# Four transformer layers on one core: later transposes, a second bank for the modulation products, and another order of loads and norm sums

## The chip, the cores and the metric

One core of one Trainium2 chip runs the whole program. The metric is the device time of one execution in microseconds (us), the median of the runs shown. TensorE (PE in the profile), VectorE (DVE), ScalarE (ACT), GpSimd (POOL) and SyncE (SP) are the engines of the core; each has its own queue of instructions.

## The reference, cut to what matters

256 latent tokens `x` and 256 context tokens `ctx`, 2048 wide, go through two layers with modulation, and the latent tokens then through two more. All in float32.

```python
# layers 0 and 1 (l = 0, 1)
mod = silu(c) @ w_mod[l] + b_mod[l];  shift, scale, gate = split(mod, 3)      # for x
cmod = silu(c_ctx) @ w_mod[l] + b_mod[l]                                      # the same for ctx
h = rmsnorm(x, norm_g[l]) * (1 + scale) + shift                              # hc from ctx
u = h @ w_in                                                                 # also uc
y = concat([mixer_1(u), mixer_2(u)]) * silu(u_gate)
x = x + gate * (y @ w_o[l])                                                  # ctx too, in layer 0
# layers 2 and 3
h = rmsnorm(x, norm)
u = h @ w_in
y = concat([mixer_1(u), mixer_2(u)]) * silu(u_gate)
x = x + y @ w_out
```

The mixers are eight kinds of attention (a to h in the kernel): a and b in layer 0, c and d in layer 1, e and f in layer 2, g and h in layer 3. Mixer e picks its keys by an indexer: sixteen small query heads `iq`, rotated, are multiplied with one key head `ik`, and the best 64 keys of each query are kept.

## The kernel before

The weights (some 390 MB) are streamed once. The unit of streaming is a **group**: 256 rows of a weight matrix, 512 columns wide, 0.5 MB. SP loads it into one of `RAW` = 6 buffers `raw`; ACT copies it, rounded, to `w_hi` (line 1046); DVE subtracts to get the rest, `w_lo` (line 1321); both lie in rings of `SPLIT` = 4. The two together stand for the float32 weight. A group is split `AHEAD` = 3 groups before its use, and its ring place is free when TensorE is done with the group four before it.

TensorE works on a group in **quanta**. For an activation product (kinds `u`, `gate`, `lat`, `res`) a quantum is one tile of 128 tokens: 2 rows of K times 3 products (lines 1851 to 1853: hi by hi, hi by lo, lo by hi), 6 matmuls of 512 columns into one of four banks `pp0` to `pp3`. A group has as many quanta as its chunk has token tiles, 4 in layer 0, 2 later. For a modulation product (kind `mod`) a group is one quantum of 4 matmuls (lines 1846, 1847), 4 rows of output in bank `Y`. A **chunk** is 512 columns of output over all K, 8 groups as a rule; `T` is its number of token tiles.

The order of everything is a table of slots. `Work.layers` writes the list of quanta, one to a slot (1644). `Plan.schedule` puts all other work at slots of that list: `evac` (the copy out of a bank, and for a gate chunk the Silu, line 1111), `store`, `cols` (modulation rows turned to columns, line 1863, in bank `O`), `bias`, the attention of each head (`attend`), `x_turn` and `y_turn` (activations transposed by TensorE, then split to `hT_hi` by ACT and `hT_lo` by DVE), `gated` (the multiplication of `y` by the Silu of the gate, line 1368). Each engine walks the slots in order and issues what is its own, at TensorE the events of a slot ahead of its quantum. Where an operand comes from another engine it waits on a semaphore, with all that is queued behind it. `Plan.turns` gives each use of a PSUM bank its turn; a use waits until the turn before is freed.

The places that the change touches:

- **Start.** `setup` of ACT issues the loads of `x` and `ctx` (2 MB each) into `xy`; SP issues the constants, `c`, `c_ctx` and the groups. The squares of `x` (`sq_x`, line 1118) are at slots 6, 8, 10 and 12. Modulation chunks scale0_n and shift0_n (n = 0 to 3) come as pairs, 16 groups; behind the pairs n = 1, 2, 3 come 2, 2 and 4 groups of `b_q0`, the first activation chunk. Four `x_turn` of layer 0 (line 1883) start 2 slots behind each shift0_n.
- **Modulation.** Each chunk adds up in bank `Y`; the next one waits until ACT has copied it to `rows` (line 1084).
- **Layer 0 to 1.** The chunk out0_3 has groups 0 to 7 with tiles 0 to 3 each; the square sums of the new `x`, the root on POOL (line 979) and the scaled identity (`diag`, line 1408) come at its end; then `x_turn` of layer 1 (line 1888).
- **Gated rows.** In layers 1 to 3, `y_to_columns` puts `gated` one slot behind a gate chunk, and the two `y_turn` (line 1912, bank `pp3`) one and two slots behind that. There are 12 such places with two `y_turn` each. The columns made are used in the out chunks, which start behind the fourth gate chunk.
- **Indexer.** `i_rope` (lines 1510 to 1513) rotates `iq` on DVE at slots base+10 to base+16, `i_turn` (line 2031, bank `pp3`) transposes it from base+15, `ik_turn` (line 2038) at base+16, `i_dots` from base+21.

Of the kernel before, what the change touches and what calls it, by code (L numbers as in the profile page):

```python
# [111 lines left out]
class Chunk:  # L112

    def __init__(self, name, kind, w, c0, W, T, ks=None, lhs="h", dst=None, dcol=None, layer=0, ycol=None, block=None, row=None, scaled=None):
        self.name, self.kind, self.w, self.c0, self.W, self.T = name, kind, w, c0, W, T
        self.ks = list(range(KT_)) if ks is None else ks
        self.lhs, self.dst, self.dcol, self.layer, self.ycol = lhs, dst, c0 if dcol is None else dcol, layer, ycol
        self.block, self.row, self.scaled = block, row, scaled
        self.groups = []

class Group:

    def __init__(self, n, ch, j, q0):
        self.n, self.ch, self.j, self.q0 = n, ch, j, q0
        self.ks = ch.ks[GROUP * j:GROUP * j + GROUP]
        self.quanta = 1 if ch.kind == "mod" else ch.T
        self.q1 = q0 + self.quanta

class Work:

    def __init__(self):
        self.groups, self.slots, self.chunks, self.C = [], [], [], {}
        self.layers()
        self.NQ = len(self.slots)
        self.NS = self.NQ + 40
        self.banks()

    def put(self, ch, j):
        g = Group(len(self.groups), ch, j, len(self.slots))
        self.groups.append(g)
        self.slots += [(g, t) for t in range(g.quanta)]
# [5 lines left out]
        ch.q1 = g.q1  # L150

    def run(self, ch, mods=(), each=0):

        mods = list(mods)
        for j in range(len(ch.ks) // GROUP):
            self.put(ch, j)
            for _ in range(each):
                if mods:
                    self.put(*mods.pop(0))
        return mods  # L160

    def layers(self):
# [22 lines left out]
        for n in range(4):  # L185
            mod1 = self.run(Chunk(f"out0_{n}", "res", "w_o0", 512 * n, 512, 4, ks=turned, layer=0), mod1, 3 if n == 1 else 2)
# [36 lines left out]
    def banks(self):  # L223

        i = half = 0
# [33 lines left out]
class Plan:  # L259
# [81 lines left out]
    def schedule(self):  # L341
        C, add = self.W.C, self.add
        for ch in self.W.chunks:
            for t in range(ch.T):
                add(ch.q1 - ch.T + t + 1, "evac", ch.name, t)
                if ch.kind == "u" and t % 2:
                    add(ch.q1 - ch.T + t + 2, "store", ch.name, t // 2)
# [4 lines left out]
            if ch.kind == "res":  # L352
                for t in range(ch.T):
                    add(ch.q1 - ch.T + t + 2, "sq", ch.layer, int(ch.name[-1]), t)
# [36 lines left out]
        add(q1 + 2, "sums", "n1", 1)  # L391
        add(q1 + 2, "root", "n1", 1)
        add(q1 + 3, "diag", 2, 4)
        for p in range(8):
            add(q1 + max(0, p - 2), "x_turn", 1, 2 * p, 0)
# [81 lines left out]
    def y_to_columns(self, l, done):  # L477
        for n in range(4):
# [3 lines left out]
            for p in (2 * n, 2 * n + 1):  # L482
                self.add(s + 1 + p % 2, "y_turn", l, 2 * p, 0)

    def turns(self):
# [17 lines left out]
        for q, todo in enumerate(self.at):  # L503
            for e in todo:
# [15 lines left out]
                elif name == "x_turn":  # L520
                    l, K, t = key
                    if l == 0:
                        use(f"X{K % 2}", *e)
                    else:
                        use(f"X{K // 2 % 2}" if l == 1 else ("X1", "Y")[K // 2 % 2], *e)
                elif name == "y_turn":
                    use(f"X{key[2]}" if key[0] == 0 else "pp3", *e)
                elif name == "gate":
                    take("X0", *e)
                    if self.W.C[key[0]].T == 4:  # L530
                        take("X1", *e)
# [33 lines left out]
def build(nc, D, out):  # L565
# [36 lines left out]
    with ExitStack() as ctx:  # L602
# [227 lines left out]
        def _(sp):  # L830
# [3 lines left out]
            for g in groups:  # L834
                if g.n >= RAW:
# [13 lines left out]
        def _(pool):  # L849
# [12 lines left out]
            def bias(name):  # L862
# [7 lines left out]
                elif ch.layer == 1:  # L870
                    pool.wait_ge(filled["X0"], left["X0", ("gate", f"out0_{n}")])
                    pool.wait_ge(filled["X1"], left["X1", ("gate", f"out0_{n}")])
# [166 lines left out]
        def _(act):  # L1039
# [27 lines left out]
            def evac(name, t):  # L1067
# [3 lines left out]
                act.wait_ge(quanta, ch.q1 - ch.T + t + 1)  # L1071
                b = ch.bank[t]
                src, done = bank[b], freed[b]
                if ch.kind == "mod":
# [4 lines left out]
                    else:  # L1079
                        r, s = row_at("gate", ch.row)  # L1080
                        if ch.layer == 1:
                            act.wait_ge(filled["X0"], left["X0", ("gate", f"out0_{ch.row}")])
                            act.wait_ge(filled["X1"], left["X1", ("gate", f"out0_{ch.row}")])
# [102 lines left out]
            def gate(name):  # L1186
# [5 lines left out]
                for v in range(2 if ch.T == 4 else 1):  # L1192
                    act.wait_ge(filled[f"X{v}"], left[f"X{v}", ("gate", name)])
                    act.activation(gateB[:, v, :], pX[:, v, :], ACT.Copy).then_inc(freed[f"X{v}"], 1)
# [110 lines left out]
            for g in groups[:AHEAD]:  # L1305
                split(g)
            for q, todo in enumerate(plan.at):
# [3 lines left out]
                if q < NQ and slots[q][1] == 0 and slots[q][0].n + AHEAD < len(groups):  # L1311
                    split(groups[slots[q][0].n + AHEAD])
# [3 lines left out]
        def _(dve):  # L1316
# [16 lines left out]
            def evac(name, t):  # L1333
# [7 lines left out]
                dve.wait_ge(quanta, ch.q1 - ch.T + t + 1)  # L1341
                if ch.layer < 2:
                    v = t // 2
                    dve.wait_ge(*freed_from(f"X{v}", ("gate", name)))
# [428 lines left out]
            for g in groups[:AHEAD]:  # L1773
                split(g)
            for q, todo in enumerate(plan.at):
# [3 lines left out]
                if q < NQ and slots[q][1] == 0 and slots[q][0].n + AHEAD < len(groups):  # L1779
                    split(groups[slots[q][0].n + AHEAD])  # L1780
# [3 lines left out]
        def _(pe):  # L1784
# [45 lines left out]
            def quantum(g, t):  # L1830
# [12 lines left out]
                for k, K in enumerate(g.ks):  # L1843
                    a, z = g.j == 0 and k == 0, g.q1 == ch.q1 and k == GROUP - 1
                    if ch.kind == "mod":
                        pe.matmul(pY[0:4, 0:ch.W], cT[:, K, :], hi[:, k, :], start=a, stop=False)  # L1846
                        ins = pe.matmul(pY[0:4, 0:ch.W], cT[:, K, :], lo[:, k, :], start=False, stop=z)  # L1847
# [8 lines left out]
            def cols(name):  # L1856
# [3 lines left out]
                pe.wait_ge(*freed_from("Y", ("acc", name, 0)))  # L1860
# [5 lines left out]
            def gate(name):  # L1866
# [3 lines left out]
                pe.wait_ge(*freed_from("Y", ("acc", f"gate{l}_{n}", 0)))  # L1870
                pe.wait_ge(gate_bias_here, 64 * (l + 1))
                for v in range(2 if ch.T == 4 else 1):
                    b = begin(f"X{v}", "gate", name)
                    c = C_SEL + 2 + 128 * v
                    pe.matmul(b, keep[r:r + 5, c:c + 128], rows[r:r + 5, s, :], start=True, stop=True).then_inc(filled[f"X{v}"], 1)
# [247 lines left out]
```

## Time and profile before

| | |
|---|---|
| median of 3 runs | 2709.29 us (2704.67 to 2714.11) |
| the profiled execution | 2709.09 us, its span 2707.3 us |
| mean granted TensorE clock | 0.981 |
| busy: PE, PE weight loads, DVE, ACT, POOL | 95%, 74%, 52%, 48%, 8% |
| DMA | 464.80 MB, mean 172 GB/s |

### The profile page before, as it was taken

Reading aid. Unit: us, or ns where it says so; the run is one execution under the profiler, and the core shown is the slowest. Engines: PE = TensorE matmul, PEld = TensorE weight load, DVE = VectorE, ACT = ScalarE, POOL = GpSimd, SP = SyncE. Lnnn points to the kernel's source line nnn. Section 1 sums busy time; section 2 is a strip of 40 time slices with the busy share of each in tenths; the row PEclk is TensorE's granted clock in tenths of the full one; section 3 lists DMA queues with packets and bytes.
Section 4 is the critical chain, followed back from the end, with each engine's and each line's share of the span. In section 5 each row is a group of like instructions: output and inputs, shape, how many; then the busy total and the mean of one; then the engine's idle time right before and its main releaser. Section 6 shows DMA issues by size and latency. Waiting matters only on the chain. (4 is left out here: it accounts for less than half of the span.)

```text
span 2707.3 us, 32472 instructions
## 1 busy us (share of the span) xinstructions
PE 2572.9 (95%) x12228; PEld 2009.2 (74%) x12228; DVE 1412.3 (52%) x2245; ACT 1298.0 (48%) x1967; POOL 221.1 (8%) x314
## 2 busy tenths in 40 slices
PE   6999999999999999999999999999988999999888
PEld 2566777777778766677777677977877887888776
DVE  6644444455553555475565545566554544444454
ACT  6644333334443444464454444545555445654543
POOL 1000001001000000000112100101110001101100
PEclk9999999999999999999999999999998999999999
DMA  9667534333222665557545444755554566567543
GB/s 323 241 219 233 184 101 124 102 97 110 86 82 86 227 221 186 175 182 240 158 154 176 128 140 163 229 165 189 173 181 134 186 208 214 175 191 232 166 155 133
DMA packets 230091, 464.80 MB, mean 172 GB/s; under 512 B 17346, under 2 KB 42240, under 8 KB 228656
## 3 DMA queue, kind: packets, MB, share of 16 engines
q1 hardware_dynamic: 208560, 390.73, 44.8%
q0 software_dynamic: 20832, 67.81, 7.9%
q10 hardware_dynamic: 544, 4.19, 0.4%
q8 instruction: 98, 1.61, 0.2%
q14 instruction: 57, 0.47, 0.1%
HBM read 431.89 MB, written 30.77 MB: 171 GB/s over the span
## 5 line engine op out<-in xcount | busy, mean ns | idle before, releaser
L1321 DVE TENSOR_TENSOR w_lo<-raw,w_hi 128x1024 fp32r<-128x1024 f32 (+4 forms) x762 | 898.5, 1194 | 1018.8 <-ACT w_hi L1046 1017.1
L1851 PE MATMUL pp<-w_hi,hT_hi 128*128 128x512 f32 (+3 forms) x2904 | 1176.1, 405 | 2.9 <-DVE w_lo L1321 2.2
L1853 PE MATMUL pp<-w_hi,hT_lo 128*128 128x512 f32 (+3 forms) x2904 | 1120.5, 386 | 0.0
L1852 PE MATMUL pp<-w_lo,hT_hi 128*128 128x512 f32 (+3 forms) x2904 | 1119.3, 385 | 0.0
L1046 ACT ACTIVATE w_hi<-raw 128x1024 fp32r<-128x1024 f32 (+4 forms) x762 | 772.6, 1030 | 702.3 <-PE pp L1853 673.8
L1851 PEld LDWEIGHTS pp<-w_hi,hT_hi 128*128 128x128 f32 x2904 | 551.1, 190 | 144.3 <-issue 42.2
L1853 PEld LDWEIGHTS pp<-w_hi,hT_lo 128*128 128x128 f32 x2904 | 549.6, 189 | 107.0
L1852 PEld LDWEIGHTS pp<-w_lo,hT_hi 128*128 128x128 f32 x2904 | 551.8, 190 | 96.3 <-issue 7.2
L1846 PE MATMUL pY<-w_hi,cT 128*4 128x512 f32 x384 | 158.6, 413 | 24.9 <-DVE w_lo L1321 12.3
L1847 PE MATMUL pY<-w_lo,cT 128*4 128x512 f32 x384 | 157.9, 411 | 0.0
L1202 ACT ACTIVATE arena<-pY 128x512 f32<-128x512 f32 (+2 forms) x114 | 62.1, 545 | 139.9 <-PE pY L2005 108.5
L881 POOL DMA_DIRECT2D scratch_u<-ust x46 | 33.8, 735 | 943.7 <-ACT ust L1106 943.7
L1846 PEld LDWEIGHTS pY<-w_hi,cT 128*4 128x4 f32 x384 | 33.5, 87 | 85.2 <-DVE w_lo L1321 29.7
L2018 PEld LDWEIGHTS pO<-arena 128*128 128x128 f32 x640 | 85.6, 191 | 8.6 <-issue 0.7
L2018 PE MATMUL pO<-arena 128*128 128x128 f32 x640 | 87.4, 275 | 0.5 <-issue 0.5
L2005 PE MATMUL pY<-keep,arena 128*128 128x128 f32 x392 | 63.4, 275 | 14.8 <-ACT arena L1224 5.9
L2005 PEld LDWEIGHTS pY<-keep,arena 128*128 128x128 f32 x392 | 48.2, 140 | 35.7 <-issue 16.4
L1847 PEld LDWEIGHTS pY<-w_lo,cT 128*4 128x4 f32 x384 | 33.5, 87 | 53.3 <-issue 10.0
L1106 ACT ACTIVATE ust<-pp,stat 128x512 f32<-128x512 f32 (+3 forms) x86 | 56.2, 662 | 26.6 <-PE pp L1853 26.4
L1212 ACT ACTIVATE arena<-pX,stat 128x512 f32<-128x512 f32 (+1 forms) x64 | 36.6, 578 | 67.2 <-DVE stat L1594 67.2
L1984 PE MATMUL pX<-arena 128*128 128x512 f32 (+1 forms) x128 | 58.7, 540 | 0.0
L1912 PE MATMUL pp<-keep,xy 128*128 128x128 f32 x96 | 21.0, 359 | 36.9 <-DVE xy L1368 34.8
(269 smaller groups left out, 1739.2 us busy)
## 6 DMA issues: line engine op xcount, KB each, us to landing
raw<-in_w_mod_dram SPq DMA_DIRECT2D x192, 512.0 KB, 4.9
raw<-in_w_in_dram SPq DMA_DIRECT2D x168, 512.0 KB, 3.6
raw<-in_e_w_in_dram SPq DMA_DIRECT2D x104, 512.0 KB, 3.6
raw<-in_w_o_dram SPq DMA_DIRECT2D x64, 512.0 KB, 3.7
raw<-in_o_w_in_dram SPq DMA_DIRECT2D x64, 512.0 KB, 3.8
raw<-in_w_out_dram SPq DMA_DIRECT2D x64, 512.0 KB, 3.6
raw<-in_w_in_dram SPq DMA_DIRECT2D x56, 440.0 KB, 3.5
scratch_u<-ust POOLq DMA_DIRECT2D x35, 512.0 KB, 3.8
```

The source lines that it names most:

```text
L1046: act.activation(w_hi[:, g.n % SPLIT, 0:n], raw[:, g.n % RAW, 0:n], ACT.Copy).then_inc(hi_done, 1)
L1106: ins = act.activation(ust[:, 2 * half + t % 2, 0:ch.W], src[:, 0:ch.W], ACT.Copy, scale=scale)
L1202: return act.activation(dst, src, ACT.Copy, scale=scale)
L1321: dve.tensor_tensor(w_lo[:, g.n % SPLIT, 0:n], raw[:, g.n % RAW, 0:n], w_hi[:, g.n % SPLIT, 0:n].bitcast(F32), ALU.subtract).then_inc(lo_d ...
L1846: pe.matmul(pY[0:4, 0:ch.W], cT[:, K, :], hi[:, k, :], start=a, stop=False)
L1847: ins = pe.matmul(pY[0:4, 0:ch.W], cT[:, K, :], lo[:, k, :], start=False, stop=z)
L1851: pe.matmul(dst, hT_hi[:, kk, o:o + P], hi[:, k, :], start=a, stop=False)
L1852: pe.matmul(dst, hT_hi[:, kk, o:o + P], lo[:, k, :], start=False, stop=False)
L1853: ins = pe.matmul(dst, hT_lo[:, kk, o:o + P], hi[:, k, :], start=False, stop=z)
L1984: ins = pe.matmul(b[:, 0:w], QT[:, h.qi % 2, qs], KT[:, h.kv % 2, x.k0:x.k1], start=True, stop=m != "d")
L2005: ins = pe.transpose(b[:, 128 * k:128 * k + 128], e[:, 128 * k:128 * k + 128], ident)
L2018: ins = pe.matmul(b[:, 0:128], p[:, 128 * k:128 * k + 128], V[:, h.kv % 2, k0 + k, :], start=k == 0, stop=k == w - 1)
```

## The change

`x` and `ctx` are loaded by SP behind the first six groups. The squares of `x` go to slots 12 to 15 and what hangs on them 3 slots later. The groups of `b_q0` come one at a time behind single modulation chunks, the last two behind all. Modulation chunks take banks `Y` and `X1` in turn; what used `X1` in layer 0's and layer 1's transposes and gates uses `O` instead. The last three groups of out0_3 are worked by token tile: tiles 0 and 1 of all three, then tiles 2 and 3. The transposes of gated rows come 3 and 4 slots later, those of the indexer 3 slots later (keys 4), and the indexer's products and all of mixer e with them 3 slots later.

```diff
+    def quantum(self, g, t):
+        self.slots.append((g, t))
+        g.q1 = g.ch.q1 = len(self.slots)
+        g.ch.end[t] = len(self.slots)
+    def tokens_first(self, ch, js):
+        last = []
+        for j in js:
+            g = Group(len(self.groups), ch, j, len(self.slots))
+            self.groups.append(g)
+            ch.groups.append(g)
+            last.append(g)
+            for t in (0, 1):
+                self.quantum(g, t)
+        for g in last:
+            for t in (2, 3):
+                self.quantum(g, t)
...
         for n in range(4):
-            for ch in (scale0[n], shift0[n]):
+            for m, ch in enumerate((scale0[n], shift0[n])):
                 self.run(ch)
-            for j in ((), (0, 1), (2, 3), (4, 5, 6, 7))[n]:
-                self.put(b_q0, j)
+                if n:
+                    self.put(b_q0, 2 * n - 2 + m)
+        for j in (6, 7):
+            self.put(b_q0, j)
...
-            mod1 = self.run(Chunk(f"out0_{n}", "res", "w_o0", 512 * n, 512, 4, ks=turned, layer=0), mod1, 3 if n == 1 else 2)
+            ch = Chunk(f"out0_{n}", "res", "w_o0", 512 * n, 512, 4, ks=turned, layer=0)
+            mod1 = self.run(ch, mod1, 3 if n == 1 else 2, 5 if n == 3 else None)
+        self.tokens_first(ch, (5, 6, 7))
...
             if ch.kind == "mod":
-                ch.bank = ["Y"]
+                ch.bank = [("Y", "X1")[n % 2]]
+                n += 1
...
-            add(6 + 2 * t, "sq_x", t)
-        add(14, "sums", "n0", 0)
-        add(14, "root", "n0", 0)
-        add(15, "diag", 0, 4)
+            add(12 + t, "sq_x", t)
+        add(17, "sums", "n0", 0)
+        add(17, "root", "n0", 0)
+        add(18, "diag", 0, 4)
...
-                add(C[f"shift0_{n}"].q1 + 2 + k, "x_turn", 0, 4 * n + k, 0)
+                add(C[f"shift0_{n}"].q1 + (2 if n else 4) + k, "x_turn", 0, 4 * n + k, 0)
...
-        q1 = C["out0_3"].q1
-        add(q1, "sums", "n1", 0)
-        add(q1, "root", "n1", 0)
-        add(q1, "diag", 0, 2)
+        q1, lat = C["out0_3"].q1, C["out0_3"].end[1]
+        add(lat + 2, "sums", "n1", 0)
+        add(lat + 2, "root", "n1", 0)
+        add(lat + 3, "diag", 0, 2)
...
-            add(q1 + max(0, p - 2), "x_turn", 1, 2 * p, 0)
+            add(q1 + max(-1, p - 2), "x_turn", 1, 2 * p, 0)
...
-            add(base + 15 + 4 * (n // 2) + n % 2, "i_turn", n)
-        add(base + 16, "ik_turn")
-        dots = base + 21
+            add(base + 18 + 4 * (n // 2) + n % 2, "i_turn", n)
+        add(base + 20, "ik_turn")
+        dots = base + 24
...
-                self.add(s + 1 + p % 2, "y_turn", l, 2 * p, 0)
+                self.add(s + 4 + 2 * (p % 2), "y_turn", l, 2 * p, 0)
...
             for g in groups:
+                if g.n == RAW:
+                    sp.dma_start(xy[:, 0:2, :], D["x"][0].rearrange("(t p) n -> p t n", p=P)).then_inc(x_here, 16)
+                    sp.dma_start(xy[:, 2:4, :], D["ctx"][0].rearrange("(t p) n -> p t n", p=P)).then_inc(x_here, 16)
                 if g.n >= RAW:
                     sp.wait_ge(lo_done, g.n - RAW + 1)
...
             def setup():
-                act.dma_start(xy[:, 0:2, :], D["x"][0].rearrange("(t p) n -> p t n", p=P)).then_inc(x_here, 16)
-                act.dma_start(xy[:, 2:4, :], D["ctx"][0].rearrange("(t p) n -> p t n", p=P)).then_inc(x_here, 16)
```

The splits of a group are still issued when the group four before it is done, which with the reordered tiles is kept in a number of its own (`split_at`).

How the instructions move. First SP at the start of the program, where the groups of w_mod are modulation and those of e_w_in are `b_q0`, later `b_q1`. Before:

```order
L831 DMA keep<-in_per_part_dram 128x770
L833 DMA arena<-in_c_dram 16x128
L833 DMA arena<-in_c_ctx_dram 16x128
L839 DMA raw<-in_w_mod_dram 128x2x512 x32
L839 DMA raw<-in_e_w_in_dram 128x2x512 x2
L839 DMA raw<-in_w_mod_dram 128x2x512 x16
```

And now:

```order
L860 DMA arena<-in_c_ctx_dram 16x128
L869 DMA raw<-in_w_mod_dram 128x2x512 x6
L863 DMA xy<-in_x_dram 128x2x2048
L864 DMA xy<-in_ctx_dram 128x2x2048
L869 DMA raw<-in_w_mod_dram 128x2x512 x18
L869 DMA raw<-in_e_w_in_dram 128x2x512
L869 DMA raw<-in_w_mod_dram 128x2x512 x8
L869 DMA raw<-in_e_w_in_dram 128x2x512
```

The two loads of tokens stand behind six groups on SP's queue, ahead of the seventh, and a `b_q0` group now stands behind every 8 groups of modulation from the 24th on.

Second, ACT at the fourth gate chunk of layer 2, y2_3, with its Silu (ust<-ust) and the first halves of the two `y_turn` (hT_hi<-pp). Before:

```order
L1106 ACTIVATE ust<-pp,stat 128x512 x2
L1111 ACT_TABLE_LOAD
L1111 ACTIVATE ust<-ust 128x1024
L1046 ACTIVATE w_hi<-raw 128x1024
L1170 ACTIVATE hT_hi<-pp 128x2x256
L1046 ACTIVATE w_hi<-raw 128x1024
L1170 ACTIVATE hT_hi<-pp 128x2x256
```

And now:

```order
L1134 ACTIVATE ust<-pp,stat 128x512 x2
L1139 ACT_TABLE_LOAD
L1139 ACTIVATE ust<-ust 128x1024
L1076 ACTIVATE w_hi<-raw 128x1024 x3
L1198 ACTIVATE hT_hi<-pp 128x2x256
L1076 ACTIVATE w_hi<-raw 128x1024
L1198 ACTIVATE hT_hi<-pp 128x2x256
```

Two more groups are split between the Silu and the first transposed rows; the place of the Silu and of the first split behind it is the same.

Third, TensorE where layer 0 ends and layer 1 begins (pp products, and the token transposes of layer 1 at line 1888, now 1921). Before:

```order
L1851 MATMUL pp<-w_hi,hT_hi 128x512
L1852 MATMUL pp<-w_lo,hT_hi 128x512
L1853 MATMUL pp<-w_hi,hT_lo 128x512
L1888 MATMUL pX<-arena,xy 128x128 x12
L1851 MATMUL pp<-w_hi,hT_hi 128x512
```

And now:

```order
L1886 MATMUL pp<-w_hi,hT_lo 128x512
L1921 MATMUL pX<-arena,xy 128x128 x4
L1921 MATMUL pO<-arena,xy 128x128 x4
L1884 MATMUL pp<-w_hi,hT_hi 128x512
L1885 MATMUL pp<-w_lo,hT_hi 128x512
L1886 MATMUL pp<-w_hi,hT_lo 128x512
L1884 MATMUL pp<-w_hi,hT_hi 128x512
L1885 MATMUL pp<-w_lo,hT_hi 128x512
L1886 MATMUL pp<-w_hi,hT_lo 128x512
L1921 MATMUL pX<-arena,xy 128x128 x4
```

Of the first three transposed pairs, two now stand ahead of the last quantum of layer 0 and one behind it.

## Rows read from the trace of the kernel before

**Rows 1.** The page: busy time; engine, us (share of the span) xinstructions.
```profile
PE 2572.9 (95%) x12228; PEld 2009.2 (74%) x12228; DVE 1412.3 (52%) x2245; ACT 1298.0 (48%) x1967; POOL 221.1 (8%) x314
```
**Rows 2.** Waits of PE: engine line <- releaser: us in total, times, longest.
```profile
PE pp L1912 <- DVE xy L1368: 34.8, 10, 4.4
...
PE pY L1846 <- ACT rows L1084: 12.1, 6, 3.4
```
**Rows 3.** Timeline at y2_3: start, us, engine line op out<-in [idle before <-releaser].
```profile
2082.48 0.39 PE L1853 MATMUL pp<-w_hi,hT_lo 128*128 128x512 f32 x1
...
2082.87 1.06 ACT L1111 ACTIVATE ust<-ust 128x1024 f32<-128x1024 f32 x1
2083.16 0.39 PE L1853 MATMUL pp<-w_hi,hT_lo 128*128 128x512 f32 x1
...
2084.90 1.23 DVE L1321 TENSOR_TENSOR w_lo<-raw,w_hi 128x1024 fp32r<-128x1024 f32 x1 [4.38 <-ACT w_hi L1046]
2086.05 1.22 DVE L1368 TENSOR_TENSOR xy<-xy,ust 128x1024 f32<-128x1024 f32 x1
2087.41 1.09 PE L1912 MATMUL pp<-keep,xy 128*128 128x128 f32 x4 [3.87 <-DVE xy L1368]
```
**Rows 4.** Windows behind waits: stretch, length, busy (x) of PE to POOL, PEclk, DMA, GB/s.
```profile
1599.00:1603.00 4.00, 3.42 (x10) 2.79 (x11) 1.84 (x3) 1.55 (x2) 0.00 (x0) 0.50 0.38 131
...
2609.00:2613.00 4.00, 3.75 (x15) 3.27 (x16) 1.84 (x3) 1.55 (x2) 0.00 (x0) 0.61 0.38 131
1771.00:1775.00 4.00, 3.90 (x13) 3.25 (x14) 3.97 (x6) 0.81 (x2) 0.00 (x0) 0.50 0.40 131
```
**Rows 5.** Timeline of PE: a gated transpose behind another user of bank pp3.
```profile
2581.84 0.66 PE L1912 MATMUL pp<-keep,xy 128*128 128x128 f32 x4 [0.75 <-ACT arena L1202]
```
**Rows 6.** Timeline of PE at the indexer's first transpose.
```profile
1771.10 1.09 PE L2031 MATMUL pp<-keep,xy 128*128 128x128 f32 x4 [4.19 <-DVE xy L1513]
```
**Rows 7.** Timeline of PE where layer 1 begins.
```profile
1158.69 5.46 PE L1888 MATMUL pX<-arena,xy 128*128 128x128 f32 x24 [4.02 <-DVE arena L1408]
1163.80 0.77 PE L1851 MATMUL pp<-w_hi,hT_hi 128*128 128x512 f32 x1
...
1165.77 1.05 PE L1888 MATMUL pX<-arena,xy 128*128 128x128 f32 x8
```
**Rows 8.** Timeline at two chunk ends of layer 1's modulation.
```profile
953.70 0.58 ACT L1084 ACTIVATE rows<-pY 4x512 f32<-4x512 f32 x1
...
954.39 1.02 PE L1863 MATMUL pO<-keep,rows 5*128 5x2 f32 x8 [2.11 <-issue]
...
1006.78 0.39 PE L1846 MATMUL pY<-w_hi,cT 128*4 128x512 f32 x1 [1.00 <-ACT rows L1084]
```
**Rows 9.** Timeline of the start: the first matmul on weights, the seventh group's split.
```profile
16.38 0.59 PE L1846 MATMUL pY<-w_hi,cT 128*4 128x512 f32 x1 [7.96 <-DVE w_lo L1321]
...
24.14 1.06 ACT L1046 ACTIVATE w_hi<-raw 128x1024 fp32r<-128x1024 f32 x1 [0.29 <-DMA raw<-in_w_mod_dram]
```
**Rows 10.** Windows of the start; columns as in group 4.
```profile
10.00:20.00 10.00, 2.14 (x5) 0.43 (x6) 2.64 (x3) 3.17 (x3) 0.00 (x0) 1.00 1.03 399
...
30.00:40.00 10.00, 7.55 (x22) 3.35 (x23) 5.87 (x7) 9.31 (x11) 0.00 (x0) 0.58 0.93 321
```
**Rows 11.** Timeline of ACT and DVE: squares of x; an x_turn of layer 0.
```profile
32.33 1.91 ACT L1118 ACTIVATE arena<-xy 128x2048 f32<-128x2048 f32 x1
...
117.03 0.43 DVE L1424 CAST hT_hi<-arena 128x512 fp32r<-128x512 f32 x1 [2.77 <-ACT arena L1152]
117.49 0.69 DVE L1425 TENSOR_TENSOR hT_lo<-arena,hT_hi 128x512 fp32r<-128x512 f32 x1
```
**Rows 12.** Timeline of PE: modulation begins behind two b_q0 groups, twice; then gate0.
```profile
87.95 0.40 PE L1846 MATMUL pY<-w_hi,cT 128*4 128x512 f32 x1
...
126.67 0.40 PE L1846 MATMUL pY<-w_hi,cT 128*4 128x512 f32 x1
...
181.24 0.40 PE L1846 MATMUL pY<-w_hi,cT 128*4 128x512 f32 x1
```

More of the change, by code:

```diff
@@ L118, in __init__ @@
         self.block, self.row, self.scaled = block, row, scaled
-        self.groups = []
+        self.groups, self.end = [], {}
 class Group:
@@ L139, in __init__ @@
         self.banks()
+        for g in self.groups[SPLIT:]:
+            g.split_at = self.groups[g.n - SPLIT].q1
     def put(self, ch, j):
@@ L149, in put, with run @@
         ch.groups.append(g)
-        ch.q1 = g.q1
-    def run(self, ch, mods=(), each=0):
+        for t in range(g.quanta):
+            self.quantum(g, t)
[3 more added lines that the diff above has]
+        g.ch.end[t] = len(self.slots)
+    def run(self, ch, mods=(), each=0, upto=None):
         mods = list(mods)
-        for j in range(len(ch.ks) // GROUP):
+        for j in range(len(ch.ks) // GROUP if upto is None else upto):
             self.put(ch, j)
@@ L1070, in evac @@
                     return
-                act.wait_ge(quanta, ch.q1 - ch.T + t + 1)
+                act.wait_ge(quanta, ch.end[t])
                 b = ch.bank[t]
@@ L1191, in gate @@
                     act.wait_ge(*freed_from(prev.bank[-1], ("acc", prev.name, prev.T - 1)))
-                for v in range(2 if ch.T == 4 else 1):
-                    act.wait_ge(filled[f"X{v}"], left[f"X{v}", ("gate", name)])
-                    act.activation(gateB[:, v, :], pX[:, v, :], ACT.Copy).then_inc(freed[f"X{v}"], 1)
+                for v, b in enumerate(("X0", "O")[:ch.T // 2]):
+                    act.wait_ge(filled[b], left[b, ("gate", name)])
+                    act.activation(gateB[:, v, :], bank[b], ACT.Copy).then_inc(freed[b], 1)
             def front_copy(which, m, n):
@@ L1306, in _ @@
                 split(g)
+            ahead = AHEAD
             for q, todo in enumerate(plan.at):
@@ L1310, in _ @@
                         mine[e[0]](*e[1:])
-                if q < NQ and slots[q][1] == 0 and slots[q][0].n + AHEAD < len(groups):
-                    split(groups[slots[q][0].n + AHEAD])
+                while ahead < len(groups) and groups[ahead].split_at <= q:
+                    split(groups[ahead])
+                    ahead += 1
         @block.vector
@@ L1778, in _ @@
                         mine[e[0]](*e[1:])
-                if q < NQ and slots[q][1] == 0 and slots[q][0].n + AHEAD < len(groups):
-                    split(groups[slots[q][0].n + AHEAD])
+                while ahead < len(groups) and groups[ahead].split_at <= q:
+                    split(groups[ahead])
+                    ahead += 1
         @block.tensor
@@ L1843, in quantum @@
                 for k, K in enumerate(g.ks):
-                    a, z = g.j == 0 and k == 0, g.q1 == ch.q1 and k == GROUP - 1
+                    a, z = g.j == 0 and k == 0, g is ch.groups[-1] and k == GROUP - 1
                     if ch.kind == "mod":
-                        pe.matmul(pY[0:4, 0:ch.W], cT[:, K, :], hi[:, k, :], start=a, stop=False)
-                        ins = pe.matmul(pY[0:4, 0:ch.W], cT[:, K, :], lo[:, k, :], start=False, stop=z)
+                        dst = bank[ch.bank[0]][0:4, 0:ch.W]
+                        pe.matmul(dst, cT[:, K, :], hi[:, k, :], start=a, stop=False)
+                        ins = pe.matmul(dst, cT[:, K, :], lo[:, k, :], start=False, stop=z)
                         continue
@@ L1869, in gate @@
                 r, s = row_at("gate", n)
-                pe.wait_ge(*freed_from("Y", ("acc", f"gate{l}_{n}", 0)))
+                pe.wait_ge(*freed_from(C[f"gate{l}_{n}"].bank[0], ("acc", f"gate{l}_{n}", 0)))
                 pe.wait_ge(gate_bias_here, 64 * (l + 1))
-                for v in range(2 if ch.T == 4 else 1):
-                    b = begin(f"X{v}", "gate", name)
+                for v, name_ in enumerate(("X0", "O")[:ch.T // 2]):
+                    b = begin(name_, "gate", name)
                     c = C_SEL + 2 + 128 * v
-                    pe.matmul(b, keep[r:r + 5, c:c + 128], rows[r:r + 5, s, :], start=True, stop=True).then_inc(filled[f"X{v}"], 1)
+                    pe.matmul(b, keep[r:r + 5, c:c + 128], rows[r:r + 5, s, :], start=True, stop=True).then_inc(filled[name_], 1)
             def x_turn(l, K, t0):
```

36 lines of the change are left out of this document (19 added, 17 removed).

## The prediction

> **What bounds the kernel now.** The page comes first: TensorE is busy for 2572.9 us of a span of 2707.3 us, VectorE for 52%, ScalarE for 48% [rows 1]. TensorE is the bound, and an edit that removes no matmul can give only two things: the 134.4 us in which TensorE has no work, and the time it loses at the lower clock. So the next view is the list of TensorE's own waits. Its top line is the transposes of gated rows (line 1912) waiting for the multiplication on VectorE: 34.8 us in 10 waits, the longest 4.4. Lower down stand the modulation products waiting for ScalarE's copy out of bank Y, 12.1 us in 6 [rows 2]. The third view is the timeline around one such wait. At y2_3 the Silu ends at 2083.93, a split stands between it and the multiplication on both engines, the multiplication runs from 2086.05 to 2087.27, and the transpose starts at 2087.41 after 3.87 us idle [rows 3]. The fourth view, windows, shows what follows: TensorE works, but at a granted clock of 0.50 to 0.63, which is the 1.2 GHz level for all or most of the stretch. There are nine such stretches behind gated transposes, 3 to 4 us long, the first and last of which are shown, and one behind the indexer's wait [rows 4].
>
> A quantum is six matmuls. The third and sixth start at 2082.48 and 2083.16 [rows 3], 0.68 us apart, so a matmul takes a step of 0.227 us and a quantum 1.36 us.
>
> **The change, part by part.** The sum is made against the profiled execution, 2709.1 us. The median is 2709.3, so nothing has to be shifted.
>
> *Gated transposes.* They move 3 slots back (the second of each pair 4). Three quanta are 4.1 us. ScalarE's and VectorE's order up to the multiplication is the same, so it ends when it did, while TensorE works on. Of the ten waits nine are of 3.2 to 4.4 us, so at most 0.3 us is left of any: 34.2 us are saved. With the idle time goes the low clock behind it. Summing length times (1 minus clock) over the nine stretches gives 17.4 us, between 1.5 and 3.1 each. The cover is the three quanta, whose weights are split already. The columns are first needed in the out chunk, for the last pair 5 slots behind its new place, so no consumer gets late. What is paid: bank pp3 is shared with the query and key transposes of mixers d to h. In the new table four y_turn stand in one slot behind a front transpose (before: two), and three front transposes follow a y_turn by one slot. The only such wait on a list of before is 0.75 us [rows 5]; the other end is a full hand-over, ScalarE's 0.60 and VectorE's 0.69 us copy, some 1.6 us with the steps between. Seven at 0.75 are 5 us, seven at 1.6 are 11. I take 5. Part: 34.2 + 17.4 - 5 = 46.6 us.
>
> *Indexer.* The first transpose waits 4.19 us for a rotation [rows 6], then comes 4 us at half clock [rows 4], worth 2.0. Three slots are again 4.1 us. Gain 6.2 us. Mixer e, its scores and selection move 3 slots with it; its heads still end ahead of the first gate chunk that needs them, so I cost that at nothing, between -2 and +2 (the waits around the attention of e are below 1.2 us each).
>
> *Layer 0 to 1.* TensorE stops at 1154.67 (4.02 us ahead of 1158.69) and begins layer 1's product at 1163.80: 9.1 us for 24 transpose records, of which 8 alone take 1.05 us [rows 7]. So 3.1 us is work and 6.0 us idle, bank waits and low clock. In the new order five quanta (6.8 us) lie between the last product of the latent tiles and the first transposes. The chain of sums, root and diag took 3.4 us from the last square to the scaled identity, and about 6 with the squares and one split ahead of it. So it fits, barely. The quantum between the transposes covers the copies. Gain 6.0 us; between 2 and 7.
>
> *Second bank.* In layer 1's modulation two waits of about 1.0 us for the copy go, one of which is the third row of [rows 8]. Where another product stands between chunk end and `cols`, it is `cols` that waits, 2.11 us, for the same copy, because ScalarE gets to it only at 953.70 [rows 8]. Those two stay. Gain 2.0 us. The waits of this kind in layer 0 are in the next part.
>
> *Start.* The first matmul on weights is at 16.38, because 4.2 MB of tokens shared the DMA engines with the first group [rows 9]. Now six groups come first, and the first matmul should be near 10. But that is given back: by the seventh group the same bytes have been asked for (0.4 + 4.2 + 7 times 0.52 MB = 8.3 MB), and at the 399 GB/s of the window [rows 10] it landed at 24.1 before [rows 9]. It lands at 24 to 25 now. TensorE will idle for about 10 us between the sixth and the seventh group, and start again at the low clock (0.58 in the window of such a restart [rows 10]).
> On one point a rule bears. The Trainium skill, "DMA: Bandwidth & Descriptors", section "Queues, rings and completion order", says that each DMA engine takes turns between queues packet by packet, and drains one ring in order. By it the seventh group now waits for all of both token loads, and a load on ScalarE's queue would have let it through at half rate. That speaks against the new place. No run shows it yet. By either, the sum up to the seventh group is the same bytes.
> The squares at slots 12 to 15 make ScalarE the pace there: 1.91 + 0.2 for each [rows 11] and 1.06 for a split [rows 9], 3.2 us a slot, to slot 16 near 45. Then the x_turn slots go at VectorE's pace, 0.43 + 0.69 [rows 11] + 1.23 [rows 3] = 2.35 us, to slot 24 near 60. A `b_q0` group is 4 quanta, 5.45 us, and the chunk behind it is 8.4: three groups split ahead, the others at 1.2 us each. With two `cols` and two x_turn of 1.0 us each, the second `b_q0` group ends near 82.4, where before it ended at 87.95 [rows 12] with two x_turn more done. Gain 3.6 us.
> From there a round of 16 modulation groups and two of `b_q0` took 126.67 - 87.95 = 38.7 us [rows 12]; TensorE's own work in it is 16 x 0.92 + 10.9 + 4 + 2 = 31.6. The new order lets splits and loads catch up twice a round. I get 11.6 for the chunk whose first slots carry two x_turn, 8.4 for the other, 10.9, 2 and 2: 34.9. Two rounds gain 7.6. Part: 11.2 us. Ends: 0, if the rounds only follow the loads, and 26, if no wait is left but those up to the seventh group.
>
> Sum: 46.6 + 6.2 + 6.0 + 2.0 + 11.2 = 72.0 us; 2709.1 - 72.0 = **2637.1 us**.
>
> **Rivals.**
> *The waits move, half of the largest part returns.* The multiplication comes later once TensorE no longer stops: VectorE and ScalarE lose the pauses in which they caught up. For it: one split stands ahead of the multiplication [rows 3]. Against it: both are at about half load [rows 1]. Half of 51.6 stays: 2637 + 26 = 2663.
> *The start gets worse.* The tokens hold up the seventh group and the squares bunch up: idle 10 us more, part -10 instead of +11: 2658.
> *The start goes better.* Rounds near TensorE's own work, part 26: 2622.
> *Slower.* The hand-over of bank pp3. 24 y_turn now stand among front transposes; if each stopped TensorE as long as the longest wait for VectorE, 4.4 us, they would cost 106 us and the time would be 2637 + 106 = 2743. It decides from 72/24 = 3.0 us a turn. Against it: 0.75 us is what the trace shows [rows 5], and 17 of 24 have no neighbour.
> *The change does little.* If the multiplication were released by something that comes later too (the split of a group whose place is freed later), the waits would follow TensorE: within 0.3%. Against it: that split's group was freed a quantum ahead.
>
> **The numbers.** A measurement can tell about 0.3%, 8 us, from no change. Forecast 0.62; half of it returned 0.17; start worse 0.08; start better 0.09; slower 0.02; nothing 0.02. The range goes from 2617 (start better, and 5 us more of the small parts) to 2667 (half returned, and a few us more) and leaves out about 0.15. Faster by over 0.3%: 0.96; within: 0.02; slower: 0.02.
>
> **What would show it.** In the profile after: no line of gated transposes waiting for the multiplication above 3 us in total; granted clock 1.00 in the windows behind these places; the indexer's wait gone; layer 1's first product within 5 us of the end of layer 0's last one but for one quantum; two `cols` waits of 2 us still there; TensorE idle for some 10 us before the seventh group, and gate0's first product near 170 instead of 181.24 [rows 12]. Wrong it is if the multiplication ends more than 4.1 us behind the end of the chunk, if new waits on bank pp3 sum to over 12 us, or if the rounds keep 38 us.

## The result, and the profile after

The changed kernel takes 2668.5 us (median of 4 runs, 2665.2 to 2672.0); the kernel before 2711.7 us (median of 4 runs). The ratio is 0.9849, 95% interval 0.9826 to 0.9872: faster by 1.5%, 41 us by the ratio and 43 by the medians, where 72 were predicted and 2667 was the edge of the range. The profiled execution is one of 2672.0 us, 37.1 less than that of before, and the places below are read from it.

The page after, busy time, answers to [rows 1]:

```profile
PE 2561.0 (96%) x12228; PEld 1999.4 (75%) x12228; DVE 1407.8 (53%) x2245; ACT 1296.1 (49%) x1967; POOL 220.6 (8%) x314
```

TensorE's idle time fell from 134.4 to 109.2 us (2670.2 - 2561.0); the other 12 of the 37 us are work that took less time, as the mean granted clock rose from 0.981 to 0.985. The list of TensorE's waits after answers to [rows 2] (engine, bank, line <- releaser: us in total, times, longest):

```profile
PE pY L1879 <- DVE w_lo L1351: 18.1, 5, 10.3
PE pO L1896 <- issue: 9.4, 8, 3.2
PE pp L1995 <- DVE hT_lo L1471: 8.9, 3, 5.4
PE pY L2038 <- ACT arena L1257: 8.0, 6, 2.9
...
PE pY L2038 <- DVE arena L1670: 3.4, 1, 3.4
...
PE pp L1945 <- DVE arena L1516: 1.6, 2, 0.8
PE pp L1945 <- ACT arena L1230: 1.5, 2, 0.7
```

The line of gated transposes (now 1945) waiting for the multiplication, 34.8 us in 10, is gone. In its place stand lines that belong to attention: the query transposes (1995) wait for `hT_lo` of line 1471, which is the second half of a gated transpose leaving bank pp3, and the transposes of probabilities (2038) wait for exp (1257) and for what VectorE makes of it (1670). The matmul that starts a chunk gives the ledger by stretches. Each figure is a difference of two starts in one trace; e1 to e12 are the experiments below. The two stretches left out change little: c_q0 to y1_0 takes 267.7 to 270.9 us in all of these traces and e6 to e9, out3_1 to the end 76.7. One trace is one draw: e1 has the order of the kernel before in the first two rows, and differs from it by 1.3 and 6.1 us there.

| from, to the first matmul of | before | after | e1 | e2 | e3 | e4 | e5 | e10 | e12 |
|---|---|---|---|---|---|---|---|---|---|
| span's start, gate0_0 | 181.2 | 177.5 | 182.5 | 178.3 | 179.4 | 176.1 | 179.2 | 175.2 | 175.6 |
| gate0_0, c_q0 (rest of layer 0) | 982.6 | 975.3 | 988.7 | 972.7 | 974.0 | 972.4 | 976.7 | 966.1 | 967.8 |
| y1_0, out1_1 (gate chunks of layer 1) | 191.4 | 184.6 | 183.1 | 191.7 | 181.8 | 180.8 | 182.4 | 183.1 | 180.8 |
| out1_1, y2_0 (indexer, mixer e) | 334.4 | 328.9 | 330.3 | 329.0 | 328.8 | 328.9 | 328.8 | 327.8 | 327.8 |
| y2_0, out2_1 | 152.3 | 144.5 | 144.2 | 150.1 | 140.2 | 139.3 | 131.0 | 142.9 | 131.0 |
| out2_1, y3_0 (mixer g) | 366.2 | 367.8 | 367.8 | 366.0 | 368.2 | 369.1 | 367.7 | 367.8 | 357.4 |
| y3_0, out3_1 | 154.2 | 145.6 | 145.5 | 154.1 | 136.0 | 138.9 | 135.6 | 145.6 | 135.6 |

The three stretches of gate chunks shrank by 6.8 + 7.8 + 8.6 = 23.2 us, against 46.6 predicted. Inside them the gain is uneven: at the three places behind the fourth gate chunk, where the out chunk runs and no attention is beside it, 6.6, 6.8 and 5.4 us; at the other nine 4.4 us together. The timeline at one of the nine, y2_1, shows why (start, us, engine, line, [idle before <- releaser]). ScalarE first:

```profile
1993.60 0.68 ACT L1134 ACTIVATE ust<-pp,stat 128x512 f32<-128x512 f32 x1
1994.30 1.28 ACT L1139 ACT_TABLE_LOAD   x1
1995.60 1.06 ACT L1139 ACTIVATE ust<-ust 128x1024 f32<-128x1024 f32 x1
1996.56 1.99 ACT L1076 ACTIVATE w_hi<-raw 128x1024 fp32r<-128x1024 f32 x2
1998.57 1.28 ACT L1257 ACT_TABLE_LOAD   x1
2004.25 0.40 ACT L1257 ACTIVATE arena<-arena,stat 128x128 f32<-128x128 f32 x1 [4.40 <-DVE stat L1651]
...
2005.14 1.04 ACT L1076 ACTIVATE w_hi<-raw 128x1024 fp32r<-128x1024 f32 x1
2006.09 0.57 ACT L1198 ACTIVATE hT_hi<-pp 128x512 fp32r<-128x512 f32 x1
```

VectorE in the same stretch:

```profile
1998.78 1.22 DVE L1398 TENSOR_TENSOR xy<-xy,ust 128x1024 f32<-128x1024 f32 x1
...
2000.45 1.22 DVE L1351 TENSOR_TENSOR w_lo<-raw,w_hi 128x1024 fp32r<-128x1024 f32 x1
2001.58 0.68 DVE L1528 TENSOR_TENSOR arena<-arena 128x512 f32<-128x512 f32 x1
...
2003.58 0.28 DVE L1651 CUSTOM_DVE_ANT_0 arena<-pX,arena 128x128 f32<-128x128 f32 x1
...
2006.21 1.22 DVE L1351 TENSOR_TENSOR w_lo<-raw,w_hi 128x1024 fp32r<-128x1024 f32 x1 [2.00 <-ACT w_hi L1076]
2007.36 0.28 DVE L1670 SCALAR_TENSOR_TENSOR arena<-arena 128x128 f32<-128x128 f32 x1
...
2007.91 0.69 DVE L1471 TENSOR_TENSOR hT_lo<-pp,hT_hi 128x512 fp32r<-128x512 f32 x1
```

And TensorE, with the window behind its wait (columns as in [rows 4]):

```profile
2001.23 0.60 PE L1945 MATMUL pp<-keep,xy 128*128 128x128 f32 x4
...
2002.82 0.40 PE L1886 MATMUL pp<-w_hi,hT_lo 128*128 128x512 f32 x1
2008.65 1.11 PE L1995 MATMUL pp<-keep,arena 128*128 128x128 f32 x4 [5.44 <-DVE hT_lo L1471]
```
```profile
2008.70:2011.70 3.00, 3.00 (x10) 2.57 (x11) 0.26 (x1) 1.60 (x3) 0.00 (x0) 0.52 0.47 164
```

Read it from the end. The query transpose of head f/4 wants bank pp3. The gated transpose filled that bank at 2001.2 to 2001.8 and it is free at 2008.6, 6.8 us after it was filled, though the two copies out take 0.57 and 0.69 us: they stand in the queues of ScalarE and VectorE behind exp and the probabilities of head f/3. Those are late because the maximum stands on VectorE behind the multiplication, a split and a rotation, and the multiplication itself waited for table load, Silu and splits. TensorE then works at 0.52, half clock for nearly all of the window.

### The profile page after: what moved, and what is told of

The parts are those of the page before. It is cut to its first block and busy times, and to the rows that moved or that the text cites. A ratio compares the mean times of both kernels' runs of the same rounds, so it can differ in the third digit from the quotient of the medians.

```text
span 2670.2 us, 32472 instructions
## 1 busy us (share of the span) xinstructions
PE 2561.0 (96%) x12228; PEld 1999.4 (75%) x12228; DVE 1407.8 (53%) x2245; ACT 1296.1 (49%) x1967; POOL 220.6 (8%) x314
## 5 line engine op out<-in xcount | busy, mean ns | idle before, releaser
L1879 PE MATMUL pY<-w_hi,cT 128*4 128x512 f32 x192 | 80.4, 419 | 18.4 <-DVE w_lo L1351 18.1
L1880 PE MATMUL pY<-w_lo,cT 128*4 128x512 f32 x192 | 79.4, 414 | 0.0
L1879 PE MATMUL pX<-w_hi,cT 128*4 128x512 f32 x192 | 76.6, 399 | 2.3 <-DVE w_lo L1351 1.8
L1880 PE MATMUL pX<-w_lo,cT 128*4 128x512 f32 x192 | 76.1, 396 | 0.0
L1879 PEld LDWEIGHTS pY<-w_hi,cT 128*4 128x4 f32 x192 | 16.7, 87 | 48.6 <-DVE w_lo L1351 26.5
```

The source lines that it names most:

```text
L1879: pe.matmul(dst, cT[:, K, :], hi[:, k, :], start=a, stop=False)
L1880: ins = pe.matmul(dst, cT[:, K, :], lo[:, k, :], start=False, stop=z)
```

## The experiments

Two theories. **A, late chain:** at the places with attention, exp stands behind the Silu, its two table loads, splits and the multiplication; TensorE used to stand still meanwhile, now it gets to attention's own transposes too early. **B, bank:** gated and query transposes share pp3, and a bank is held as long as its copies stand in the queues. Each kernel ran in 5 rounds; the kernel before, beside them, gave 2712.2 (e1 to e4), 2708.6 (e5 to e8) and 2707.1 us (e9 to e12). These are three sets on three chips, and the changed kernel was not run again in them. So a difference to its 2668.5 us, or between sets, is given by the medians and, where these mislead, by the ratios to the kernel before too (0.001 is 2.7 us).

**e1, the later gated transposes alone**, in the kernel before:

```diff
-                self.add(s + 1 + p % 2, "y_turn", l, 2 * p, 0)
+                self.add(s + 4 + 2 * (p % 2), "y_turn", l, 2 * p, 0)
```

> The kernel before with the later transposes of gated rows as the only edit (3 and 4 slots). The prediction on record gives 46.6 us for it: 2709 - 47 = about 2663. Theory A (the multiplication's wait is replaced, at the eight places where attention runs beside the gate chunks, by waits of attention itself, whose exp stands behind the Silu, two table loads and splits; only places without attention gain in full): about 23 us, some 2687. If the larger start and the other parts had taken the gain away, and not the transposes, this run alone would show 46.

Measured: 2688.6 us, ratio 0.9915 (0.9902 to 0.9927), 23.6 us below the kernel before. **e2, the same line undone** in the changed kernel:

> The changed kernel with the transposes of gated rows put back one and two slots behind the multiplication. Theory A: 23 us slower than the changed kernel, about 2692. The prediction's own price: 46.6 us slower, about 2715. The other parts of the change together would then be 20 us (A) or about zero (prediction's price).

Measured: 2689.8 us, ratio 0.9923 (0.9911 to 0.9935), 21.3 us above the changed kernel's 2668.5. Both ways round the part is worth 21 to 24 us. The other parts, 2712.2 - 2689.8 = 22.4 us together, are near the 25.4 predicted for them. Most of the miss, 22 to 25 of some 30 us, is in this one term; most of the rest is at the start.

**e3, no table loads.** In layers 1 to 3:

```diff
-                    act.activation(pair, pair, ACT.Silu).then_inc(silued, 1)
+                    act.activation(pair, pair, ACT.Silu if ch.layer == 0 else ACT.Copy).then_inc(silued, 1)
```

> The changed kernel with the Silu of the gate chunks of layers 1 to 3 replaced by a plain copy on the same engine, of the same tile; the activation function is left out of the computation there. The two table loads of 1.28 us at each of the 12 places go, all else stays. Theory A: exp comes 2.6 us sooner at the places with attention, most of their waits and of the low clock behind them go: 10 to 20 us faster than the changed kernel, about 2654. Theory B (the waits are hand-overs of bank pp3 between gated and query transposes): the copies come sooner too, but the hand-overs stay: 0 to 5 us.

Measured: 2656.0 us, ratio 0.9788 (0.9773 to 0.9803), 12.5 us below the changed kernel by the medians, 16.5 by the ratios. The three stretches give 16.7 of the 23.4 us that the part lacks. (23 table loads go, from 44 to 21: one of the 12 places had no second one.) In the waits of this run the hand-over is shorter and still there:

```profile
PE pp L1995 <- DVE hT_lo L1471: 7.4, 3, 4.2
...
PE pY L2038 <- ACT arena L1257: 4.8, 5, 1.6
```

So A holds, and it feeds B: a shorter queue ahead of the copies is also a bank freed sooner.

**e4, the transposes apart.** The order of all else is kept. (Eleven of them move, by 2 to 9 slots; the expectation says seven.)

```diff
+            q = s + 4
             for p in (2 * n, 2 * n + 1):
-                self.add(s + 4 + 2 * (p % 2), "y_turn", l, 2 * p, 0)
+                while any(e[0] in ("front_q", "front_k") for k in (-1, 0, 1, 2) for e in self.at[q + k]):
+                    q += 1
+                self.add(q, "y_turn", l, 2 * p, 0)
+                q += 2
```

> The changed kernel with seven of the gated transposes of the places with attention moved 1 to 9 slots further back, so that none stands within two slots ahead of or one slot behind a query or key transpose, which use the same bank pp3. Theory B (hand-over of pp3): 10 us or more faster than the changed kernel, the waits at 1977 and 2008 us gone. Theory A: the late chain stays, and TensorE waits for it one or two slots further on instead: 0 to 4 us faster.

Measured: 2652.6 us, ratio 0.9786 (0.9773 to 0.9799), 15.9 us below the changed kernel; the three stretches give 15.7. The query transposes' waits for `hT_lo`, 8.9 us, are gone. B is the larger share, and my expectation for A alone (0 to 4) is wrong. The edit isn't quite B alone: the two copies move back with each transpose, and so leave the queues ahead of attention's work. A bank of their own for the gated transposes, at unchanged slots, would tell the two apart; it was not tried. The late chain is still there, as the waits from 1930 to 2110 us (layer 2) show:

```profile
PE pY L2042 <- DVE arena L1674: 6.9, 3, 3.4
PE pO L2058 <- issue: 1.5, 1, 1.5
PE pp L1999 <- issue: 1.3, 1, 1.3
```

**e5, Silu behind exp**, on top of e4:

```diff
+            k = ch.q1
+            while l > 1 and n < 3 and any(e[0] == "exp" for j in range(5) for e in self.at[k + j]):
+                k += 1
+            if k > ch.q1:
+                self.late.add(ch.name)
+                self.add(k, "silu", ch.name, 1)
+                s = k + 1
```

> The kernel of the run with the transposes apart, and beside it the Silu of four gate chunks in layers 2 and 3 (and its multiplication) put one slot behind the next exp instead of ahead of it. What is left in that run at these places are waits of attention's second transposes for exp or for the probabilities behind it: 1.1, 2.4, 3.4, 1.2, 2.5 and 2.9 us, 13.5 us with low clock behind them. Theory A (exp stands behind Silu, table loads and splits): at least the 2.4, 3.4, 2.5 and 2.9 go, with the low clock behind, 10 to 18 us faster than that run's 2652.6, near 2639. Rival (ScalarE and VectorE are simply full there): the waits only change places, within 4 us of 2652.6.

The gated transposes of these four places follow their multiplication, and stand 2 to 5 slots further back than in e4; what that alone gives is not known.

Measured: 2646.2 us, ratio 0.9764 (0.9742 to 0.9786). By the medians this is 6.4 us below e4, less than the 10 expected, in an interval that overlaps e4's. The stretches of layers 2 and 3, whose order alone changed, say more: 139.3 to 131.0 and 138.9 to 135.6, 11.6 us. The same window as above has left:

```profile
PE pY L2056 <- DVE arena L1688: 2.1, 2, 1.1
PE pO L2072 <- issue: 2.0, 2, 1.5
PE pY L2056 <- ACT arena L1275: 0.4, 1, 0.4
```

With both repairs the three stretches of gate chunks are 449.0 us, and 447.4 in e12, which keeps them; before they were 497.9. The whole 46.6 us was there to be had, and up to 3.9 more.

**e6, squares of x at slots 6, 8, 10, 12** (`add(6 + 2 * t, "sq_x", t)` for `add(12 + t, ...)`), in the changed kernel:

> The changed kernel with the squares of x at slots 6, 8, 10, 12, as before the change, instead of 12 to 15; all else as changed. If the bunched squares, behind which the copy of modulation rows stands, are what kept the start from its 11.2 us, the wait of 3.2 us for the rows at 46 us goes with the low clock behind it, the end of the second b_q0 group comes near 83 instead of 88, and the time is 3 to 7 us below the changed kernel. If ScalarE's total work sets the pace there, the same time within 2 us.

Measured: 2665.6 us, ratio 0.9844 (0.9823 to 0.9865): 2.9 us below the changed kernel by the medians, 1.4 by the ratios, which the intervals don't separate and which is less than the 3 to 7 expected. In the trace the wait of 3.2 us at 46 us is gone, scale0_2 starts at 85.4 instead of 89.3 and gate0_0 at 173.9. Five executions whose start is as changed have gate0_0 at 176.1 to 179.4, the two with the squares apart (this and e9) at 173.9 and 176.7. Some 1 to 3 us, then, likely and not settled.

**e7, the loads of tokens on ScalarE's queue again:**

> The changed kernel with the two loads of tokens issued by ScalarE at the start, as before the change. By the sum on record (the same bytes up to the seventh group) it is the same up to about slot 8: first matmul near 16 again, no idle of 10 us behind the sixth group, and the time within 2 us of the changed kernel. If the place on SP's queue is what costs, as the rule on queues says, it is faster by 3 to 8 us; if the earlier first matmul is worth something, slower by as much.

Measured: 2668.3 us, ratio 0.9850 (0.9829 to 0.9872), the same. The first matmul on weights is at 16.29 instead of 9.96, gate0_0 at 177.43 instead of 177.54. That the sum up to the seventh group is the same bytes was right, and the earlier first product is worth nothing. Of the rule weighed in the prediction (the Trainium skill, "DMA: Bandwidth & Descriptors", "Queues, rings and completion order") the direction shows: the seventh group's split waits for its load until 25.81 in the changed kernel, behind both loads of tokens, and starts at 24.25 here. No time hung on it.

**e8, the groups of b_q0 in the places of before:**

> The changed kernel with the groups of b_q0 in the places of before (2, 2 and 4 behind a pair of modulation chunks). The sum on record gives the single groups 7.6 us over two rounds, and some of 3.6 ahead of them: 7 to 11 us slower than the changed kernel. If the rounds follow the loads, no difference.

Measured: 2674.2 us, ratio 0.9868 (0.9847 to 0.9890), 5.7 us above the changed kernel by the medians and 5.1 by the ratios, less than the 7 to 11 expected; gate0_0 at 184.9, 7.3 later than in the changed kernel's trace and 5.5 to 8.8 later than in the five executions with its start. The total is near the 7.6 us worked out for the single groups, but it comes from other places: 3.9 us ahead of scale0_2, 3.3 in the first round (38.7 us here, 35.4 in the changed kernel), 0.2 from scale0_3 to gate0_0.

**e9, e5 and e6 together:**

> The kernel of the run with the Silu behind exp, and beside it the squares of x at slots 6, 8, 10, 12. If the two are independent (start and gate chunks): 3 to 4 us below that run's ratio of 0.9764 to the kernel before, a ratio near 0.975, about 2642.

Measured: 2642.1 us, ratio 0.9761 (0.9737 to 0.9784). The median is 4.1 us below e5's, the ratio hardly: the squares' gain stays within the spread.

**e10, `cols` one slot later**, in the changed kernel:

```diff
-                    add(ch.q1 + 1, "cols", ch.name)
+                    add(ch.q1 + (1 if ch.name == "shift0_3" else 2), "cols", ch.name)
...
-                add(C[f"shift0_{n}"].q1 + (2 if n else 4) + k, "x_turn", 0, 4 * n + k, 0)
+                add(C[f"shift0_{n}"].q1 + (4, 3, 3, 2)[n] + k, "x_turn", 0, 4 * n + k, 0)
```

> The changed kernel with the turning of modulation rows to columns one slot later (2 instead of 1 behind the chunk, shift0_3 excepted; x_turn of the middle two pairs of layer 0 one slot later too). What is left of these waits after the change is 9.4 us in 8, with low clock behind the three longest. If the wait for ScalarE's copy of the rows is covered by one more quantum: 5 to 9 us faster than the changed kernel. If the copy is later still (it stands behind a split or squares): within 2 us.

Measured: 2655.2 us, ratio 0.9813 (0.9789 to 0.9836): 13.3 us faster than the changed kernel by the medians, 9.8 by the ratios, a little more than expected. (The same edit gives 11.8 us from e9 to e11, which ran side by side.) The waits fell from 9.4 to 2.5 us:

```profile
PE pO L1896 <- issue: 2.5, 4, 0.8
```

The rest is clock, at this place at least, where the changed kernel and e10 show (windows, columns as before):

```profile
1092.00:1100.00 8.00, 7.04 (x21) 5.88 (x22) 2.69 (x4) 1.90 (x3) 0.00 (x0) 0.59 0.60 197
```
```profile
1080.00:1096.00 16.00, 15.24 (x71) 10.72 (x70) 10.66 (x13) 8.64 (x14) 0.00 (x0) 1.00 0.56 187
```

**e11, e9 with e10's edit**, and **e12, that with the later steps of mixer g two slots back** (`g_sum` at 6 for 4, `g_less` 7, `g_exp` 8, `g_pv` 10, `g_finish` 11):

> The joined kernel (transposes apart, Silu behind exp, squares apart) with the columns of modulation one slot later. 3 to 8 us below the joined one; less than by itself, since the longest of the waits goes with the squares already.

> The kernel of the run before this one with the later steps of mixer g (its sums, exponentials and products) two slots later. The waits of TensorE for the logarithm, 7.0 us in 5, and the low clock behind the longest go: 5 to 10 us faster, if nothing else waits in their place; within 2 us if the chain behind them (exp, then the products) is what holds TensorE.

Measured: e11 2630.3 us, ratio 0.9722 (0.9699 to 0.9745), 11.8 below e9, where 3 to 8 were expected: the squares alone had taken none of it, as TensorE's waits for the columns are 9.6 us in e9 and 1.5 in e11. e12 2621.1 us (2621.1 to 2623.9), ratio **0.9685** (0.9662 to 0.9707), 9.2 below e11; the stretch with mixer g fell from 366.2 us in e11 to 357.4. The page of e12:

```profile
PE 2538.4 (97%) x12228; PEld 1985.0 (76%) x12228; DVE 1408.6 (54%) x2245; ACT 1291.0 (49%) x1965; POOL 221.2 (8%) x314
```

e12 beats both kernels: 86 us below the one before, beside which it ran, and 44 (by the ratios) to 47 below the changed one.

## Why the prediction was wrong

**The step that failed** is the price set against the gain of the gated transposes: "Seven at 0.75 are 5 us, seven at 1.6 are 11. I take 5." By what e4 gives back, the shared bank cost about 16 us, and a second price, for attention's chain, was not in the sum at all: about 6 to 12 us (e5). 46.6 + 5 - 16 - 10 is 26, where 21 to 24 were measured.

- *The gain itself was right.* The ten waits are gone. Where nothing else is near, the low clock behind them is gone too (the window from 2078 to 2082 us has 1.00), and the place gave 5.4 to 6.8 us. The 17.4 us for the low clock don't follow from stretches of 3 to 4 us: 4 us at 0.50 lose 2.0, not up to 3.1. In the trace five of the nine stay at 0.50 for 5.3 to 5.9 us behind the wait, the other four for about 3, which makes some 20 us in all. So the term was not too large.
- *"It ends when it did" was right to a hundredth.* From the end of the last matmul of y1_0 to the end of the multiplication it is 6.34 us before and after, at y2_1 7.14 and 7.15, and at none of the 12 places does it change by more than 0.01. So the sign "more than 4.1 us behind the end of the chunk" was badly put: it is 6.3 to 7.9 us in both kernels, as the transposes stood two slots behind the chunk already; with three more, five quanta, 6.8 us, lie between. The sentence "no consumer gets late" looked at one consumer only, the out chunk. The transposes of attention are TensorE's too. At y2_2 exp starts 7.02 us behind the chunk's end before and 7.03 after; at y2_1 and y3_1 it starts 2.5 us sooner (11.40 for 13.95, 8.82 for 11.30). TensorE, without the waits of 3.2 to 3.5 us at these three places, gets to what hangs on exp sooner still.
- *The upper end of pp3 was no bound.* 1.6 us is how long the copies run. The bank was held 6.8 us. The price of this shared bank was the place of its copies in the queues, and these queues were the very ones known to be late there. The waits on pp3 in the list after are 8.9 + 1.6 + 1.5 = 12.0 us, right at the 12 us set as a sign of being wrong, and some 2 of them were there before: the low clock behind a wait is not in such a sum. The count of neighbours was short by one too: in the new table four front transposes follow a y_turn by one slot, not three. The 0.75 us of [rows 5] is a hand-over in a kernel where TensorE had stood still just before.
- *The rivals.* "Half of the largest part returns", 2663, was the case, at a chance of 0.17. Its size was right and its first sentence wrong: the multiplication does not come later, what stands behind it does. "Slower" named the right bank; the price came to 16 us, not the 72 it needed.
- *Indexer:* 5.5 in its stretch (6.2 predicted), *layer 0 to 1* 7.2 (6.0): right. The last quantum of layer 0 starts at 1150.56 and layer 1's first product at 1152.82, where 9.1 us lay between the two before:

```profile
1150.56 0.48 PE L1884 MATMUL pp<-w_hi,hT_hi 128*128 128x512 f32 x1
...
1152.82 0.48 PE L1884 MATMUL pp<-w_hi,hT_hi 128*128 128x512 f32 x1
```

- *Second bank.* Predicted 2.0; the profiled pair shows about 0.5 net. The two waits for the copy are gone, and the low clock behind the `cols` waits that stay fell differently. The pair is one draw of each: from gate0_0 to c_q0 the kernel before and e1 take 982.6 and 988.7 us, the nine executions with the new order 974.1 in the mean. So 2.0 is neither shown nor refuted. The waits that I let stand were the better target: e10 and e11 show 10 to 13 us for them and those of layer 0.
- *Start.* 11.2 predicted, 3.7 in the profiled pair. The first round was right: 35.4 us (89.25 to 124.63) against 34.9. The second was not: from scale0_3 to gate0_0 it is 54.6 us before and 52.9 after, a gain of 1.7 where 3.8 was summed. Right were slot 16 "near 45" (44.7) and the idle before the seventh group, the first row here:

```profile
28.25 0.59 PE L1879 MATMUL pY<-w_hi,cT 128*4 128x512 f32 x1 [10.27 <-DVE w_lo L1351]
...
49.78 1.84 PE L1896 MATMUL pO<-keep,rows 5*128 5x2 f32 x8 [3.20 <-issue]
```

 What was missed is the second row. I counted the four squares as ScalarE's pace but not that the copy of shift0_0's rows stands behind them, so that `cols` waits 3.2 us, and half clock follows (0.50 from 50 to 54 us). The second `b_q0` group ended at 88.4 instead of 82.4.

What stays open: how the 16 and the 10 us divide exactly, since each repair shortens what the other waits for (e3 alone gave 12.5 to 16.7), how much of the 16 is the bank and how much the copies' place in the queues, and the size of the squares' share.

## What to carry to other kernels

When a wait of the bounding engine is taken away, walk the queues of the other engines *behind* the operation it waited for: all that stands there keeps its time or gains less than the wait, while the bounding engine gets to it sooner by the length of the wait. Price a shared PSUM bank by when its copies get their turn in their queues, not by how long they run; moving one user past the other's turn gave two thirds of what was missing here. Then move what makes the chain late, here the Silu with its table loads, right behind the urgent operation.

## What was unexpected

- A bank with 1.3 us of copies was held 6.8 us. The Trainium skill, "PSUM — Partial Sum Buffer", "Engine vs sequencer instructions", says that the queues of ScalarE and VectorE are strictly first in, first out. The trace agrees: ScalarE stood idle 4.40 us ahead of the exp at 2004.25, with the copy that frees the bank in its queue behind that exp.
- A wait of about 2 us cost more than itself here, and not always the same: with the `cols` waits unchanged the stretch from gate0_0 to c_q0 takes 972.4 to 976.7 us over nine profiled executions (the changed kernel, e2 to e9), and 966.1 to 967.8 in the three with `cols` later.
- A first matmul on weights 6.3 us sooner made no difference behind the start: gate0_0 comes at 177.54 with it and at 177.43 without (e7).
